# A two-block network on one core: gate and up products with the high and low activations in one 512-column pass

## The reference

```
def rms_norm_2(x, g):
    xf = x.astype(jnp.float32)
    y = xf * lax.rsqrt(jnp.mean(xf * xf, axis=-1, keepdims=True) + RMS_EPS)
    return (y * g.astype(jnp.float32)).astype(x.dtype)
def swiglu_ffn(x, w_gate, w_up, w_down):
    return (jax.nn.silu(x @ w_gate) * (x @ w_up)) @ w_down
def second_block(x, ...):
    ...
    for layer in range(DEPTH_2):
        h = h + HALF_STEP * swiglu_ffn(rms_norm_2(h, ffn1_norm[layer]), ...)
        u = rms_norm_2(h, mix_norm[layer])
        ...
        h = h + HALF_STEP * swiglu_ffn(rms_norm_2(h, ffn2_norm[layer]), ...)
```

## Time and profile before

| | us |
|---|---|
| median of three runs | 1376.14 |
| lowest and highest run | 1373.8 and 1378.49 |
| span of the profiled execution, first to last instruction | 1372.0 |
| TensorE busy | 1342.0 (98%) |
| VectorE busy | 840.4 (61%) |
| ScalarE busy | 581.7 (42%) |
| GpSimd busy | 109.3 (8%) |

### The profile page before, as it was taken

How to read it: one execution, slowest core, us unless ns; L and a number is a source line. 1 busy time by engine, 2 the same in 40 slices (tenths; PEclk the granted TensorE clock), 3 DMA queues, 4 the chain that set the end, 5 groups by cost and what they waited for, 6 DMA issues and landing times.

```text
span 1372.0 us, 20927 instructions
## 1 busy us (share of the span) xinstructions
PE 1342.0 (98%) x8618; PEld 1210.9 (88%) x8618; DVE 840.4 (61%) x950; ACT 581.7 (42%) x689; POOL 109.3 (8%) x141
## 2 busy tenths in 40 slices
PE   7999999999999999997999999999999999999997
PEld 6878878889999888996999988899998977999986
DVE  6465775766666555757666546556664555666653
ACT  5354566533444434215444434344443435444440
POOL 4133011000000011220000000000000110100000
PEclk9999999999999999999999999999999989999999
DMA  9544544455655655202465564665545511565540
GB/s 309 184 152 148 164 140 168 167 201 184 187 182 182 215 172 186 92 1 90 156 192 184 182 209 155 194 203 182 185 157 181 203 43 62 169 213 183 182 158 31
DMA packets 164900, 224.67 MB, mean 164 GB/s; under 512 B 7473, under 2 KB 105857, under 8 KB 164832
## 3 DMA queue, kind: packets, MB, share of 16 engines
q1 hardware_dynamic: 163168, 220.23, 48.7%
q0 software_dynamic: 1648, 3.47, 1.0%
q10 hardware_dynamic: 16, 0.00, 0.0%
HBM read 222.62 MB, written 1.05 MB: 163 GB/s over the span
## 4 chain that ended last, share of the span: by engine, by line
PE 96%; DVE 2%; ACT 1%; DMA 0%; issue 0%; POOL 0%; POOLq 0%; DVEq 0%; SPq 0%; ACTq 0%
PE acc L580 15%; PE acc L581 14%; PE acc L582 14%; PE acc L615 13%; PE acc L611 13%; PE acc L613 13%; PE att L848 4%; PE tp L636 1%; DVE wlo L1252 1%; PE acc L950 1%; ACT whi L980 0%; PE att L705 0%; PE acc L938 0%; PE att L938 0%; DMA h<-in_x_dram 0%; PE acc L890 0%
## 5 line engine op out<-in xcount | busy, mean ns | idle before, releaser
L1252 DVE TENSOR_TENSOR wlo<-raw,whi 128x2048 fp32r<-128x2048 f32 x208 | 474.5, 2288 | 143.3 <-ACT whi L980 143.3
L980 ACT ACTIVATE whi<-raw 128x2048 fp32r<-128x2048 f32 x208 | 390.8, 1910 | 113.7 <-PE acc L582 102.4
L611 PE MATMUL acc<-aT_hi,whi 128*128 128x256 f32 x1536 | 435.5, 284 | 0.0
L615 PE MATMUL acc<-aT_hi,wlo 128*128 128x256 f32 x1536 | 434.6, 283 | 0.0
L613 PE MATMUL acc<-aT_lo,whi 128*128 128x256 f32 x1536 | 434.6, 283 | 0.0
L613 PEld LDWEIGHTS acc<-aT_lo,whi 128*128 128x128 f32 x1536 | 294.8, 192 | 0.2
L611 PEld LDWEIGHTS acc<-aT_hi,whi 128*128 128x128 f32 x1536 | 294.8, 192 | 0.2
L615 PEld LDWEIGHTS acc<-aT_hi,wlo 128*128 128x128 f32 x1536 | 294.8, 192 | 0.0
L580 PE MATMUL acc<-whi,aT_hi 128*128 128x512 f32 x480 | 192.4, 401 | 8.3 <-DVE aT_lo L1677 6.2
L581 PE MATMUL acc<-whi,aT_lo 128*128 128x512 f32 x480 | 188.7, 393 | 0.0
L582 PE MATMUL acc<-wlo,aT_hi 128*128 128x512 f32 x480 | 188.4, 393 | 0.0
(11 more groups left out here) (261 smaller groups left out, 1216.9 us busy)
## 6 DMA issues: line engine op xcount, KB each, us to landing
raw<-in_ffn_w_gate_dram SPq DMA_DIRECT2D x88, 512.0 KB, 4.0
raw<-in_ffn_w_up_dram SPq DMA_DIRECT2D x88, 512.0 KB, 5.1
raw<-in_ffn_w_down_dram SPq DMA_DIRECT2D x88, 512.0 KB, 4.6
raw<-in_w_in_dram SPq DMA_DIRECT2D x72, 512.0 KB, 4.8
raw<-in_conv_w_pw_dram SPq DMA_DIRECT2D x24, 512.0 KB, 4.6
raw<-in_w_kv_dram SPq DMA_DIRECT2D x16, 512.0 KB, 4.9
raw<-in_ret_w_o_dram SPq DMA_DIRECT2D x8, 512.0 KB, 4.5
raw<-in_diff_w_o_dram SPq DMA_DIRECT2D x8, 512.0 KB, 4.6
```

What stands on the lines that cost most here:

```text
L611: mm_(dst, whi[:, slot, cols], aT_hi[:, kt, :], start=half == 0 and j == 0 and n == 0, stop=False, skip_group_check=True)
L615: last = mm_(dst, wlo[:, slot, cols], aT_hi[:, kt, :], start=False, stop=half == 1 and j == SLAB_K - 1, skip_group_check=True)
L980: A_(whi[:, slot, :], raw[:, slot, :], ACT.Copy).then_inc(hi_ready, 1)
L1252: V.tensor_tensor(wlo[:, slot, :], raw[:, slot, :], whi[:, slot, :].bitcast(F32), ALU.subtract)\
```

## The change

`aT_hi` and `aT_lo` become two halves of one buffer `aT`, side by side for each contraction block. In chunks 1 to 10 of each network `wide_slab` takes the place of `turned_slab`: for each block of weights, `wlo` by `aT_hi` as a matmul of 256 columns, then `whi` by `aT_hi` and `aT_lo` together as one matmul of 512 columns. It makes 16 x 2 matmuls of a slab in place of 16 x 3. The low activations' product stands in its own half of the bank, so each 128 hidden features take a whole bank, and a chunk takes two pairs of banks, one for gate and one for up. `ffn_pair` hands out three pairs in turn (two of `acc`, and the two `att` banks). Chunk 0 stays as it was.

ScalarE copies the low half of a pair into `low_part` (`low_products`), twice a chunk, and VectorE's `summed` adds it to the other half. The gate sum is then multiplied by `rsb`; the up sum is not. The factor left out there is applied at the residual, which takes `rs_down` = 0.5 x `rs` of each token (GpSimd makes it) in place of 0.5. `spread_rs` writes to a `tp` bank in the networks. The loops over chunks are written out on all engines, and TensorE's wait at the first down slab is for one `acc_free` more.

```diff
-        aT_hi = sb("aT_hi", [P, KT, T], F32R)
-        aT_lo = sb("aT_lo", [P, KT, T], F32R)
+        aT = sb("aT", [P, KT, 2, T], F32R)
+        aT_hi, aT_lo = aT[:, :, 0, :], aT[:, :, 1, :]
...
+        def ffn_pair(name, c, up):
+
+            g = PLACE[name].g
+            ring = [acc_pair[(g + 1) % 2], att_pair, acc_pair[g % 2]]
+            return ring[(2 * (c - 1) + up) % 3]
...
+                pool.wait_ge(rs_ready, use + 1)
+                nc.gpsimd.tensor_scalar(rs_down[:, use, :], rs[:, use, :], 0.5, None, ALU.mult)\
+                    .then_inc(rs_down_ready, 1)
...
+            def wide_slab(k, name, c, half):
+
+                w = PLACE[name]
+                pe.wait_ge(lo_ready, k + 1)
+                slot = k % SLOTS
+                for up in range(2):
+                    if half == 0 and c >= 2:
+
+                        pe.wait_ge(acc_free, 2 * (w.g + c - 1) + (up - 1) + 1)
+                    for n in range(FW // P):
+                        bank = ffn_pair(name, c, up)[:, n, :]
+                        f = up * (FW // P) + n
+                        for j in range(SLAB_K):
+                            kt = 4 * half + j
+                            cols = slice(j * CW + f * P, j * CW + (f + 1) * P)
+                            mm_(bank[:, 0:T], wlo[:, slot, cols], aT_hi[:, kt, :], start=half == 0 and j == 0,
+                                stop=False, skip_group_check=True)
+                            last = mm_(bank[:, :], whi[:, slot, cols],
+                                       aT[:, kt, :, :].rearrange("p a n -> p (a n)"), start=False,
+                                       stop=half == 1 and j == SLAB_K - 1, skip_group_check=True)
+                    last.then_inc(half_done, 1)
...
-                with pe.Fori(0, (FC - 3) // 2) as it:
-                    for s in range(4):
-                        turned_slab(w.k + 4 + s, w.g + 2 + s // 2, s % 2, it)
-                for s in range(2):
-                    turned_slab(w.k + 20 + s, w.g + 10, s)
+                    if c == 0:
+                        turned_slab(w.k + s, w.g, half)
+                    else:
+                        wide_slab(w.k + s, name, c, half)
+                    if s == 2 and name in SPREADS:
+                        spread_rs(name, tp[0])
...
-                            pe.wait_ge(acc_free, 2 * (g - 1))
+                            pe.wait_ge(acc_free, 2 * (g - 1) + 1)
...
+                def low_products(c):
+                    for up in range(2):
+                        done(w.k + 2 * c + 1, up)
+                        act.wait_ge(acc_free, 2 * (w.g + c))
+                        A_(low_part[:, up, :, :], ffn_pair(name, c, up)[:, :, T:CW], ACT.Copy)\
+                            .then_inc(low_copied, 1)
...
+                for s in range(4, 2 * FC):
+                    if s % 2 == 0:
+                        low_products(s // 2 - 1)
+                        hidden(s // 2 - 2)
+                    else:
+                        silu(s // 2 - 1)
+                    cast(w.k + s + AHEAD)
...
-                def scaled(c, it=None):
+                def summed(c):
 
                     k = w.k + 2 * c + 1 if c else w.k + 2
...
+                    gate, up = act_out[:, c % 2, :, :], hid[:, c % 2, :, :]
+                    dve.wait_ge(lo_ready, k + AHEAD + 1)
+                    if c:
+                        dve.wait_ge(low_copied, copied + 2 * c - 1)
+                        V.tensor_tensor(gate, ffn_pair(name, c, 0)[:, :, 0:T], low_part[:, 0, :, :], ALU.add)\
                             .then_inc(acc_free, 1)
...
+                        dve.wait_ge(acc_free, 2 * (w.g + c) + 1)
+                        V.tensor_tensor(gate, gate, spread, ALU.mult).then_inc(gate_ready, 1)
+                        dve.wait_ge(low_copied, copied + 2 * c)
+                        V.tensor_tensor(up, ffn_pair(name, c, 1)[:, :, 0:T], low_part[:, 1, :, :], ALU.add)\
+                            .then_inc(acc_free, 1)
+                    else:
+                        done(k, 1)
+                        one = [acc[w.g % 2][bank].rearrange("p (f n) -> p f n", n=T) for bank in range(2)]
+                        V.tensor_tensor(gate, one[0], spread, ALU.mult).then_inc(gate_ready, 1)
+                        dve.wait_ge(gate_ready, before + 1)
+                        V.tensor_copy(up, one[1]).then_inc(acc_free, 2)
...
-                        residual(w.g + FC, 0, 0.5, lambda t: dve.wait_ge(half_done, 2 * (w.k + 2 * FC + 5) + 1))
+                        dve.wait_ge(rs_down_ready, use + 1)
+                        residual(w.g + FC, 0, rs_down[:, use, :],
+                                 lambda t: dve.wait_ge(half_done, 2 * (w.k + 2 * FC + 5) + 1))
```

More of the change, by code:

```diff
@@ L189, in build @@
         g_out = sb("g_out", [P, D], to=second)
+        low_part = sb("low_part", [P, 2, FW // P, T], to=second)
         second.close()
@@ L584, in part, with slab @@
                 return last
-            def slab(k, g, half, Th, Tl, it=None, tokens=natural, split=None):
+            def slab(k, g, half, Th, Tl, tokens=natural, split=None):
                 if half == 0 and g >= 2:
-                    pe.wait_ge(acc_free, at(2 * (g - 1), it, 4))
-                pe.wait_ge(lo_ready, at(k + 1, it, SLOTS))
+                    pe.wait_ge(acc_free, 2 * (g - 1))
+                pe.wait_ge(lo_ready, k + 1)
                 for t in range(TT):
@@ L594, in slab, with turned_slab @@
                          half == 0, half == 1, tokens, split).then_inc(half_done, 1)
-            def turned_slab(k, g, half, it=None):
+            def turned_slab(k, g, half):
                 if half == 0:
-                    pe.wait_ge(acc_free, at(2 * (g - 1), it, 4))
-                pe.wait_ge(lo_ready, at(k + 1, it, SLOTS))
+                    pe.wait_ge(acc_free, 2 * (g - 1))
+                pe.wait_ge(lo_ready, k + 1)
                 slot = k % SLOTS
@@ L626, in spread_rs @@
                 for t in range(TT):
-                    last = mm_(att[0][:, t * P:(t + 1) * P], ones[:, :], rdiag[:, t, :], start=True, stop=True)
+                    last = mm_(bank[:, t * P:(t + 1) * P], ones[:, :], rdiag[:, t, :], start=True, stop=True)
                 last.then_inc(rsb_mm, 1)
@@ L650, in ffn_pe @@
                 w = PLACE[name]
-                for s, (c, half) in enumerate(pair_order(2)):
+                if name == "ffn1b":
+                    pe.wait_ge(rsb_ready, SPREADS.index("kv") + 1)
+                for s, (c, half) in enumerate(pair_order(FC)):
                     if s == 1:
@@ L855, in _ @@
                 pe.wait_ge(tp_lo, p1.b - 2 if s < 2 else p1.b)
-                slab(p1.k + s, p1.g + c, half, aT_hi, aT_lo, None, phase)
+                slab(p1.k + s, p1.g + c, half, aT_hi, aT_lo, phase)
                 if s == 2:
@@ L970, in _, with cast @@
             A_ = nc.scalar.activation
-            def cast(k, it=None):
+            def cast(k):
                 if k >= SLABS:
@@ L1125, in ffn_act @@
                 cast(w.k + 3 + AHEAD)
-                with act.Fori(0, (FC - 3) // 2) as it:
-                    for s in range(4):
-                        if s % 2 == 0:
-                            hidden(s // 2, it)
-                            silu(1 + s // 2, it)
-                        cast(w.k + 4 + s + AHEAD, it)
-                hidden(8)
-                silu(9)
-                cast(w.k + 20 + AHEAD)
-                cast(w.k + 21 + AHEAD)
-                hidden(9)
-                silu(10)
-                cast(w.k + 22 + AHEAD)
-                hidden(10)
+                for s in range(4, 2 * FC):
[5 more added lines that the diff above has]
+                    cast(w.k + s + AHEAD)
+                low_products(FC - 1)
+                hidden(FC - 2)
+                silu(FC - 1)
+                cast(w.k + 2 * FC + AHEAD)
+                hidden(FC - 1)
                 for s in range(1, DOWN_SLABS):
@@ L1244, in sync, with low @@
                 dve.wait_ge(dve_step, steps[0])
-            def low(k, it=None):
+            def low(k):
                 if k >= SLABS:
@@ L1523, in multiplied, with hidden @@
+                def multiplied(c):
+                    dve.wait_ge(silu_made, before + c + 1)
+                    dve.wait_ge(acc_free, 2 * (w.g + c) + 2)
                     V.tensor_tensor(hid[:, c % 2, :, :], act_out[:, c % 2, :, :], hid[:, c % 2, :, :], ALU.mult)\
                         .then_inc(hid_ready, 1)
-                def hidden(c, it=None):
-                    dve.wait_ge(hid_hi, at(before + c + 1, it, 2))
-                    tiles = slice(2 * c, 2 * c + 2) if it is None else bass.ds(it * 4 + 2 * c, 2)
+                def hidden(c):
+                    dve.wait_ge(hid_hi, before + c + 1)
+                    tiles = slice(2 * c, 2 * c + 2)
@@ L1570, in leave_ffn @@
             def leave_ffn(name, use):
+                down = dict(FFNS)[name]
                 w = PLACE[name]
```

(2 more changed lines are left out.)

126 lines of the change are left out of this document (54 added, 72 removed).

## The result

| | before | changed |
|---|---|---|
| median, us (7 runs each) | 1373.94 | 1369.56 |
| lowest to highest, us | 1373.57 to 1378.78 | 1368.4 to 1370.56 |
| ratio to before | | 0.995 (95% interval 0.9936 to 0.9964) |
| span of the profiled execution, us | 1372.0 | 1366.8 |

The changed kernel is faster by about 7 us by the ratio. The two medians lie 4.4 us apart and the two means 6.1 us, since the runs of before form two groups (five at 1373.6 to 1376.1 and two at 1378.5 and 1378.8). The forecast was 17 us and a time of 1359, with a range to 1366: the direction is right, the size is less than half, and the time lies outside the range.

What follows compares the result with a forecast made beforehand. TensorE's matmul count times start-to-start time was taken as the bound. Saving 17.1 us from the 1372.0 us span, all other terms 0, gave 1354.9, plus 4.1 between span and median: 1359.0 us, range 1354 to 1366.

Steps and rivals of the forecast that it cites:

- The reading of the bound: In the four networks TensorE is never late, so their time is matmul count times start-to-start time.
- TensorE's part: Chunks 1 to 10 of four networks: 1280 blocks each save one fixed part of 13.33 ns, 17.1 us in sum.
- pairs not 347 ns apart: Sign in the changed trace that would prove the forecast wrong: pair starts in `wide_slab` not 347 ns apart.
- Its range for a pair: Narrow plus wide matmul: at least 320 ns (no fixed part left), at most 360 ns (no gain); 346.7 taken.
- the small edits: GpSimd's extra step, the residual's factor, written-out loops and the buffer's new layout: all 0 us.
- The ring, VectorE and ScalarE: Bank freeing and both engines' chunk work: copy 0.65 us, VectorE 8.0 and ScalarE 6.3 of 11.09 us, 0 us reaching TensorE.
- The rival in which the ring becomes the bound: Two lows ahead of VectorE's gate sum stall each chunk 0.55 us, 22 us in all: 1381 us; chance 3%.
- the 13.3 ns stay with the block: Fixed part belongs to a block of weights or its columns; a pair costs 360 ns, nothing saved: 1376 us; chance 3%.
- the cheaper narrow matmul: Narrow matmul between wide ones loses its fixed part too, 13.3 ns more a block, another 17.1 us: 1342; chance 4%.
- waits eat part of it: Conversions ahead of ring steps cost 6 us over 40 chunks, the stage starts 3 us: 1368; 7% for 1363 to 1372.
- The offset: Difference between profiled span and median time, 4.1 us, added to the forecast span of 1354.9 us to give 1359.0.

Runs made afterwards that it cites:

- E10: Changed kernel with `rs_down` moved behind all other buffers, two small unused matmuls in `ffn1b`, and the wide matmul first in each pair: 1353.81 us, ratio 0.9842.

## Why the prediction was wrong

**The reading of the bound was right.** TensorE's pace times its count sets the time, and no wait came or went.

**TensorE's part was right in its price.** A pair takes 346.7 ns in three networks, 13.3 ns less than three narrow matmuls. The Trainium skill's 2.5 ns ("TensorE: Matmul & The Clock Gate", Back-to-back issue gap, which gives that formula for a single matmul on its own) would have made a pair 357.5 ns from 360, an estimate; the 346.9 ns of the three networks doesn't agree with it and decides for the rows. In `ffn1b` 304 pairs (19 slabs from slab 3 on) took 353.3 ns, so 2.0 us of the 17.1 were missed; this is the smaller of the two misses. The prediction said that what would prove it wrong were "pairs not 347 ns apart", and took one value for all networks. Its range for a pair, 320 to 360 ns, held.

**The step that failed is the one on the small edits,** which put them at nothing: "The buffer's new layout changes strides only, and the 512 columns are contiguous. All 0." I looked at the layout of `aT`, and at `rs_down` only as an instruction on GpSimd. Where the 64 bytes of `rs_down` lie was not asked. They cost 6.8 us in the down slabs (1056 matmuls, 6.67 ns each, would be 7.0), and 1.1 us in the two projections of `bT` (23.71 to 24.25 us and 24.87 to 25.46 us, 96 matmuls each). With both, -15.0 + 6.8 + 1.1 = -7.1 us, and the measured ratio gives -6.9 (-8.8 to -4.9). Between the two profiled executions the spans differ by 5.2 us. Most of the rest, 1.5 us, is between `ffn1a` and `ffn2a`, where the convolution stands (144.9 to 146.4 us): the granted clock averaged 0.80 from 615 to 640 us there and 0.86 before. That stage took between 144.7 and 147.7 us in the traces of this document.

The row that could have warned me was in the trace of before, in the projection that follows `ffn1a`, whose left operand takes every second token (`phase`, L570). Twelve of its matmuls in TensorE's timeline:

```profile
522.17 0.39 PE L580 MATMUL acc<-whi,aT_hi 128*128 128x512 f32 x1
...
524.97 0.39 PE L580 MATMUL acc<-whi,aT_hi 128*128 128x512 f32 x1
```

That is 2.80 us, 233.3 ns each, with the same widths, the same clock and no waits as in the earlier trace rows at 226.67. The fixed part was thus 13.3 ns in one place and 20.0 in another, and what differs is how the loaded operand lies in SBUF. I took 13.3 ns as the price of a matmul "whatever its width" from two stages and didn't look at a third.

**The ring, VectorE and ScalarE** went as worked out: copy 0.60 us, no wait of TensorE, 82.4 us of VectorE in the 117.2 us from slab 1 on (70%, forecast 72%). The rival in which the ring becomes the bound fell. The rival "the 13.3 ns stay with the block" fell too, since the pairs took 346.7, and so did the cheaper narrow matmul, which asked for 333. The rival "waits eat part of it" had the price 1368, close to the measured time, but by luck: TensorE has no such wait.

**The offset** of 4.1 us between span and median was the median of three runs; the profiled execution of the changed kernel was 1.7 us longer than its span, and seven runs of before have a median of 1373.94. With that the forecast would have been 1357, and the gap to the measured time larger, not smaller.

## What to carry to other kernels

When a change adds or moves a buffer, list what lies behind it in memory and what TensorE loads from there: 64 bytes cost 3% of each matmul of 512 columns here, and the same buffer put at the end cost nothing. Where a stage is bound by TensorE's pace, measure the start-to-start time in every stage, not in two, and ask of each different value what sets it. After a change, look at the stages that it doesn't touch as well: here they gave back 8 of the 15 us that the changed stage had gained. And compare totals at the same granted clock: in one stage it moved the time by as much as the whole change.

## What the runs showed of the hardware

- A matmul of 512 columns took 226.7 ns from start to start with its loaded operand in place or 256 bytes further, 233.3 ns with it 64 bytes off, 232.5 ns with 128. The Trainium skill's page "SBUF — State Buffer" (Operand start alignment) asks for a multiple of the element size and says that this is about legality and not speed; these runs add that there is a price in speed.
- With a loaded operand of every second token it was 233.3 ns in place and 230 ns with it 64 bytes off (one run).
- A matmul of 256 columns took 117.9 ns with its streamed operand 64 bytes off (one run) and 120.0 ns in place.
- A stream of wide and narrow matmuls in turn ran at 346.7 or 353.3 ns a pair with the same operands, and two small matmuls between slabs took it from the slower pace to the faster.
- In the second block's attention the granted clock fell to the level of 1.2 GHz in some executions and not in others, which moved the total by 7 to 8 us; how often it stayed up differed between the kernels (0 of 26 runs of before, 5 of 5 of E10), though the stage's code was the same.
